# Four w_mod chunks of layer 1 are multiplied between the layers, not inside the delta rule

## The chip, the cores and the metric

The kernel runs on one core of a Trainium2 chip. The metric is the device time of one execution in microseconds. The median of three runs of the kernel before is 1710.85 us (1703.96, 1710.85 and 1711.68).

## What is computed

Two layers run over 640 tokens of width 1024 (128 context tokens, 512 latent ones). Cut to what matters here, for each layer `l`:

```
mod = silu(c) @ w_mod[l] + b_mod[l]           # 6 * 1024 columns: shift1, scale1, gate1, shift2, scale2, gate2
x = x + gate1 * (mixer(rms_norm(x) * (1 + scale1) + shift1) @ w_out[l])
x = x + gate2 * experts(rms_norm(x) * (1 + scale2) + shift2)      # 16 experts, expert choice
```

Layer 0's mixer is an RG-LRU beside differential attention. Layer 1's is a chunked gated delta rule beside grouped-query attention. `scale2` and `gate2` of layer 1 are columns 4096 to 6143 of `w_mod[1]`, and nothing reads them before layer 1's second norm.

## The kernel before, in words

Everything is float32. Activations lie transposed (`xT`, `hT`: 8 tiles of 128 channels by 640 tokens). Each engine has its own hand-written program, and the order in it is the order of the Python code: there is no scheduler.

**Weights.** They pass through nine homes ("slots") of 128 x 4096 floats, 2 MB each. Slots 0 to 2 are the tensor `ring`, and slots 3 to 8 are the first 24576 columns of `arena`. SyncE (SP) issues every weight load, in the order of the list `loads`, in `load_stream`; before a load it waits until TensorE (PE) has read what lay in that slot. A chunk is 512 columns of a weight matrix, 2 MB. `w_mod` has 24 chunks, `all_mods[0]` to `all_mods[23]`. Chunks 20 to 23 are `scale2` and `gate2` of layer 1. In this text "input chunks" are those of `w_in_cd`, layer 1's input projection, taken in the order 4, 5, 0, 1, 2, 3 (chunk 5 is narrower, 1088 KB).

**Experts.** `moe_pe` runs 16 experts. An expert's three matrices take a set of three slots: set 0 is slots 3, 4, 5, set 1 is 6, 7, 8, set 2 is 0, 2, 1. The experts use the sets in the order 0, 1, 2, 0, 1, 2, 0, 1, and then 2, 0, 2, 0, 2, 0, 2, 0. So slots 6, 7 and 8 are free after the eighth expert, and the last expert (the sixteenth) is in set 0. Of each expert, PE runs line 1648 (the first two matrices), 1660 and 1665 (the third). GpSimd (POOL) adds the result to `moe_rows` in DRAM with an indirect DMA (line 1803).

**Between the layers.** After layer 0's last expert, `gather_sum_act` makes ScalarE (ACT) wait for all the adding DMAs (semaphores `y_room0` to `2`), and issue two small cache loads and four loads of `moe_rows`, a quarter of the columns each (`m_quarter0` to `3`), into `rows_m` at column 12800 of the arena. Meanwhile `sum_pe` on PE runs 12 fillers (`keep_busy`, two recorded matmuls each, whose result nobody reads), and then for each of 8 channel tiles five transposes (line 1920); VectorE (DVE) adds the tile to `xT` (lines 1351, 1354), ACT squares it (line 676), and PE sums the squares (line 1926). The norm's root, `norm_spread_pe` (lines 641, 642) and the scaling of `hT` follow, and then the first input chunk (line 762). SP issues the second and third input chunks when `m_quarter3` has come.

**The w_mod chunks.** A chunk's product is eight matmuls with 32 columns each (`mod_rows_pe`, line 493, 16 records for 8 instructions), a copy by ACT, four transposes (`mod_turn_pe`, line 504) and two or three small operations of DVE (`mod_dve`). Chunks 20 to 23 are handled by the `late_mod_*` functions inside `delta_pe`: each of the first four of the delta rule's five rounds takes one chunk, with the first half of its matmuls (`late_mod_rows(.., 0)`, line 522) between `am(j + 2)` and `am(j + 3)`, the second half between `wu(j)` and `wu(j + 1)`, and the transposes (`late_mod_turn`, line 532) behind `wu(j + 1)`.

Of the kernel before, what the change touches and what calls it, by code (L numbers as in the profile page):

```python
# [23 lines left out]
D = 1024  # L24
# [54 lines left out]
def build(nc, io, outs):  # L79
    with ExitStack() as ctx:  # L80
# [35 lines left out]
        def ar(off, *shape):  # L116
            n = 1
            for x in shape:
                n *= x
            assert off + n <= AR, (off, n)  # L120
            v = arena[:, off:off + n]
            if len(shape) == 2:
                v = v.rearrange("p (a b) -> p a b", b=shape[1])
            elif len(shape) == 3:
                v = v.rearrange("p (a b c) -> p a b c", b=shape[1], c=shape[2])
            return v
# [95 lines left out]
        def mmk(pe, out, lhs, rhs):  # L222

            for k in range(KD):
# [11 lines left out]
        chunks = [all_mods[:4] + ins[0][0:1] + all_mods[4:5] + ins[0][1:2] + all_mods[5:6] + ins[0][2:3] +  # L236
                  all_mods[6:8] + ins[0][3:4] + all_mods[8:11] + ins[0][4:5] + all_mods[11:14] + wouts[0][:1] +
                  all_mods[14:15] + wouts[0][1:] + all_mods[15:20],
                  ins[1] + all_mods[20:] + wouts[1]]
        first_slots = [0, 1, 2, 0, 1, 2, 0, 2, 1, 2, 2, 0, 2, 2, 2, 1, 2, 2, 2, 0, 1, 2, 6, 7, 0, 2, 1]  # L240

        SETS = ((3, 4, 5), (6, 7, 8), (0, 2, 1))
# [16 lines left out]
        loads = []  # L259
        for l in range(2):  # L260
            for i, c in enumerate(chunks[l]):
                s = first_slots[i] if l == 0 else i % 3 if i < 6 else i % 2
                slot_uses[s] += 1
                slot_of[c] = (s, slot_uses[s])
                loads.append((c, s, last_in_slot.get(s)))
                last_in_slot[s] = c
            for p, three in enumerate(SETS):
                for s in three:
                    slot_of["exp", l, s] = slot_uses[s]
                    slot_uses[s] += IN_SET[p]  # L270
            loads.append((("experts", l), None, dict(last_in_slot)))
            for s in range(3):
                last_in_slot[s] = ("experts", l)
        slots = [ring[:, s, :] for s in range(3)] + [ar(4096 * s, 4096) for s in range(6)]
        w_here = [S(f"w_here{s}") for s in range(9)]
# [199 lines left out]

        mrow = [ar(22360 + 512 * i, 512) for i in range(2)]
        modsum = sm[:, 616:624]
        mrow += [ar(25856 + 512 * i, 512) for i in range(2)]
        mrow_of = lambda i: mrow[i % 2 + (2 if i >= 14 else 0)]
        MOD_RAW = 26944  # L480

        def mod_rows_pe(pe, i, pair=None):
# [905 lines left out]
        idx_p = ar(26928, NE)[0:CAPP, :].bitcast(U32)  # L1388

        grow_s, grow_p = wr[:, :, :, :].rearrange("p l k e -> p (l k e)"), csil.rearrange("p k c -> p (k c)")  # L1390
        rows_m = ar(12800, NT, D)


        row_of = lambda n: ar(20480 + D * (n % 3), D)
# [416 lines left out]
        def load_stream(sp):  # L1811
            for c, s, prev in loads:
                if c[0] != "experts":
                    if prev is not None:
                        if prev[0] == "experts":
                            l = prev[1]
                            pair = 1 + SETS[2].index(s)
                            last = max(e for e in range(NE) if set_of(e) == 2)
                            sp.wait_ge(pair_full[pair], moe_base[l][pair] + (last + 1) * PER[pair])
                        else:  # L1820
                            read_by_now(sp, prev)
                    if c == chunks[0][1]:
                        sp.wait_ge(S("x_here"), 16 * NT)
                    if c == chunks[1][1]:
                        sp.wait_ge(S("m_quarter3"), 16)
                    src, n = chunk_src(c)
                    sp.dma_start(chunk(c), src.rearrange("(k p) n -> p k n", p=P)).then_inc(w_here[s], 16)
                    if c == chunks[1][2]:
                        layer1_consts_dma(sp)
                    if c == ins[0][0]:  # L1830
                        setup_late_dma(sp)
                        sp.wait_ge(S("zeroed"), 2)
                        setup_gates_dma(sp)
                    if c == wouts[c[1]][1]:

                        filled(sp, ("dyT", ST) if c[1] == 0 else ("cyT", 3))
                        sp.wait_ge(S("caches"), (48, 96)[c[1]])
                    if c in (all_mods[16], wouts[1][1]):
                        l = 0 if c == all_mods[16] else 1
                        for j in range(3):  # L1840
                            load_expert(sp, l, by_itself(0), j, False)
                        if l == 1:
                            for j in range(2):
                                load_expert(sp, 1, by_itself(FIRST.index(1)), j, False)
                else:
                    experts_stream(sp, c[1], prev)
# [45 lines left out]
                        load_expert(sp, l, in_loop(r, q), j, 2)  # L1892


        def gather_sum_act(act, l):
            for p in range(3):
                act.wait_ge(S(f"y_room{p}"), 16 + 16 * IN_SET[p])
            for pair in range(4):
                act.wait_ge(pair_free[pair], moe_base[l][pair] + NE * PER[pair])

            q = S("gqa_cache")
            act.dma_start(gk_c, io["cache_gqa_k"][0, 0].rearrange("t h d -> t (h d)")).then_inc(q, 16)
            act.dma_start(gv_c, io["cache_gqa_v"][0, 0].rearrange("t h d -> t (h d)")).then_inc(q, 16)
            for q in range(4):
                act.dma_start(rows_m[:, :, 256 * q:256 * q + 256],
                              DR["m"][:, 256 * q:256 * q + 256].rearrange("(t p) d -> p t d", p=P))\
                    .then_inc(S(f"m_quarter{q}"), 16)

        def sum_pe(pe, l):
            un = ("nrm", 1, 0)  # L1910
            acc = take(pe, un, 3)
            keep_busy(pe, acc, 12)
            for k in range(KD + 3):
                if k < KD:
                    if k % 2 == 0:
                        pe.wait_ge(S(f"m_quarter{k // 2}"), 16)
                    u = ("ms", l, k)
                    ps = take(pe, u, k % 3)
                    for t in range(NT):
                        last = pe.transpose(ps[:, t * P:t * P + P], rows_m[:, t, k * P:k * P + P], ident)  # L1920
                    finish(last, u)
                j = k - 3
                if j >= 0:
                    pe.wait_ge(S("sq"), 16 + j + 1)
                    for t in range(NT):
                        last = pe.matmul(acc[:, t:t + 1], sq_all[:, j, t * P:t * P + P], ones[:, 0:1],  # L1926
                                         start=(j == t == 0), stop=(j == KD - 1 and t == NT - 1))
            finish(last, un)
# [428 lines left out]
        def delta_pe(pe):  # L2357
# [151 lines left out]
            for i in range(5):  # L2509
                j = 2 * i  # L2510
                for s in range(1, 6):
                    for e in range(2):
                        level_w(j + e, s)

                    if s in (1, 3) and i == 0:
                        kq(TILE_ORDER[2 + s // 2])
                    elif s in (1, 3):
                        state_a(j - 2 + s // 2)
                    elif s in (2, 4) and i < 4:
                        dec(j + 1 + s // 2)  # L2520
                    elif s == 5 and i == 2:
                        kq(ST)
                    for e in range(2):
                        level_x(j + e, s)
                    if s in (1, 3) and i == 0:
                        kk(TILE_ORDER[2 + s // 2])
                    elif s in (1, 3):
                        state_b(j - 2 + s // 2)
                    elif s in (2, 4):
                        qd(j - 1 + s // 2)  # L2530
                    elif s == 5 and i == 2:
                        kk(ST)
                if i < 4:
                    am(j + 2)
                    late_mod_rows(pe, 20 + i, 0)
                    am(j + 3)
                    wu(j)
                    late_mod_rows(pe, 20 + i, 1)
                    wu(j + 1)
                    late_mod_turn(pe, 20 + i, late_row)  # L2540
                else:
                    wu(j)
                    spare()
                    wu(j + 1)
# [36 lines left out]
        def delta_act(act, step):  # L2581
# [55 lines left out]
            for i in range(5):  # L2637
# [26 lines left out]
                uw_read(j)  # L2664
                if i == 4:
                    root(3)
                else:
                    late_mod_act(act, 20 + i, late_row)
                uw_read(j + 1)
            rows_first(8)  # L2670
            square(4)
# [28 lines left out]
        def delta_dve(v, step):  # L2700
# [88 lines left out]
            for i in range(5):  # L2789
# [25 lines left out]
                if i < 4:  # L2815
                    for e in range(2):
                        x_first(j + 2 + e)
                    late_mod_dve(v, step, 20 + i)
            o_sum(v, 9, dscr3, 0)
            o_scale(3)  # L2820
            state_new(8)
# [140 lines left out]
        def _(act):  # L2962
            step = Steps(act, S("act_step"))
            setup_act(act, step)
            for l in range(2):
# [30 lines left out]
                route_act(act, step, l)  # L2996
                moe_act_run(act, l)
                if l == 0:
                    gather_sum_act(act, l)

        @block.vector
        def _(v):
            step = Steps(v, S("dve_step"))
            setup_dve(v, step)
            for l in range(2):
# [35 lines left out]
                route_dve(v, step, l)  # L3041
                moe_dve(v, step, l)
                if l == 0:
                    residual_dve(v, step, l, "ms")

        @block.gpsimd
# [66 lines left out]
```

## Time and profile before

| | us |
|---|---|
| median of 3 runs | 1710.85 |
| the profiled execution's own time | 1709.0 |
| its span in the trace | 1707.2 |
| PE busy | 1571.3 (92%) |
| DVE busy | 667.8 (39%) |
| ACT busy | 426.9 (25%) |
| POOL busy | 253.5 (15%) |

Busy times are of the whole span. Layer 0's experts end near 762 us in the trace, the stretch between the layers goes from there to 802, and the rounds of the delta rule run from about 1120 to 1310. The columns of the window views are, for each engine, busy us and in brackets the instructions; then PE's granted clock as a share of 2.4 GHz (1.00 is 2.4 GHz, 0.50 is 1.2 GHz), the mean busy share of the 16 DMA engines, and GB/s.

### The profile page before, as it was taken

How to read it: one execution, taken by the hardware profiler on the slowest of the kernel's cores; microseconds unless marked ns; L12 is line 12 of the kernel's file. 1: busy time of each engine (PE TensorE's matmuls, PEld its weight loads, DVE VectorE, ACT ScalarE, POOL GpSimd, SP SyncE). 2: the span in 40 equal slices, each digit the busy share in tenths (PEclk: the TensorE clock that was granted, in tenths of full speed). 3: DMA queues.
4: the chain of work that ended last, by engine and by line, in shares of the span. 5: the costliest groups of instructions: out<-in, count | busy, mean ns of one | idle time of the engine just before them, and what ended most of it. 6: DMA issues, size and time to landing. Idle time of an engine off the chain costs nothing.

```text
span 1707.2 us, 39998 instructions
## 1 busy us (share of the span) xinstructions
PE 1571.3 (92%) x17826; PEld 1034.9 (61%) x17826; DVE 667.8 (39%) x1414; ACT 426.9 (25%) x734; POOL 253.5 (15%) x263
## 2 busy tenths in 40 slices
PE   5999998989979999999999989988878998999996
PEld 2554434655546777766655558667666556767774
DVE  3543584751331111113039636644454134222221
ACT  3245413640311111113010236442232032000000
POOL 0000000000011111100000016155452001212211
PEclk8999999999989999997999989999999998999998
DMA  9444444025499999985121100002112617999995
GB/s 345 174 147 167 178 154 105 1 83 213 163 360 367 374 369 365 382 300 167 50 98 51 53 1 2 1 15 88 52 52 77 281 63 276 369 382 362 365 386 193
DMA packets 89932, 325.69 MB, mean 191 GB/s; under 512 B 11556, under 2 KB 17304, under 8 KB 81592
## 3 DMA queue, kind: packets, MB, share of 16 engines
q1 hardware_dynamic: 75824, 284.80, 44.3%
q0 software_dynamic: 9648, 32.65, 7.0%
q10 hardware_dynamic: 4312, 6.03, 1.0%
q8 instruction: 122, 2.00, 0.5%
q14 instruction: 26, 0.21, 0.0%
HBM read 301.30 MB, written 22.16 MB: 189 GB/s over the span
## 4 chain that ended last, share of the span: by engine, by line
PE 73%; DVE 7%; issue 3%; ACT 1%; DMA 1%; POOL 0%; POOLq 0%; DVEq 0%; ACTq 0%
PE pairs L225 19%; PE pairs L1648 17%; PE pairs L1660 7%; PE pairs L1665 3%; PE pairs L1631 2%; PE pairs L371 2%; PE pairs L1264 2%; PE pairs L2416 1%; PE pairs L2210 1%; PE pairs L2190 1%; PE pairs L1278 1%; PE pairs L2173 1%; PE pairs L1926 1%; PE pairs L762 1%; PE pairs L2427 1%
## 5 line engine op out<-in xcount | busy, mean ns | idle before, releaser
L225 PE MATMUL pairs<-hT,ring 128*128 128x128 f32 (+1 forms) x1120 | 306.1, 436 | 2.3 <-ACT hT L385 2.3
L225 PEld LDWEIGHTS pairs<-hT,ring 128*128 128x128 f32 x1120 | 170.6, 192 | 138.3 <-issue 138.2
L385 ACT ACTIVATE arena<-pairs 128x512 f32<-128x512 f32 (+6 forms) x214 | 124.7, 598 | 372.7 <-PE pairs L225 126.6
L1648 PE MATMUL pairs<-arena 128*64 128x80 f32 x5120 | 186.8, 235 | 9.7 <-issue 8.0
L1648 PEld LDWEIGHTS pairs<-arena 128*64 128x64 f32 x5120 | 181.7, 138 | 19.7 <-issue 17.2
L225 PE MATMUL pairs<-ring,hT 128*128 128x512 f32 (+1 forms) x448 | 178.5, 558 | 0.0
L225 PEld LDWEIGHTS pairs<-ring,hT 128*128 128x128 f32 x448 | 84.6, 191 | 90.3 <-issue 87.3
L1723 DVE TENSOR_TENSOR arena<-arena,pairs 128x160 f32<-128x160 f32 x64 | 20.6, 321 | 251.6 <-PE pairs L1648 251.6
L1648 PE MATMUL pairs<-arena,ring 128*64 128x80 f32 x3072 | 111.0, 233 | 5.8 <-issue 5.8
L1648 PEld LDWEIGHTS pairs<-arena,ring 128*64 128x64 f32 x3072 | 107.9, 137 | 12.1 <-issue 12.1
L385 DVE COPY arena<-pairs 128x512 f32<-128x512 f32 (+7 forms) x37 | 25.2, 703 | 127.5 <-PE pairs L225 120.8
L1660 PE MATMUL pairs<-arena 128*64 128x512 f32 x320 | 74.8, 610 | 0.0
L1351 DVE SCALAR_TENSOR_TENSOR xT<-pairs,modt,xT 128x512 f32<-128x512 f32 x24 | 18.0, 750 | 142.1 <-PE pairs L225 124.7
L1688 ACT ACTIVATE arena<-pairs 128x640 f32<-128x640 f32 x32 | 22.5, 704 | 193.1 <-PE pairs L1631 193.1
L1693 ACT ACTIVATE arena<-pairs 128x320 f32<-128x320 f32 x32 | 14.0, 437 | 226.2 <-PE pairs L1648 226.2
L371 PE MATMUL pairs<-cst 128*128 128x512 f32 x110 | 60.8, 698 | 3.2 <-DVE hT L1744 2.3
L676 ACT ACTIVATE arena<-xT 128x640 f32<-128x640 f32 x32 | 23.3, 736 | 157.9 <-DVE xT L1354 138.5
L2139 POOL TENSOR_TENSOR arena<-arena,sm 128x640 f32<-128x640 f32 (+1 forms) x40 | 43.1, 1081 | 93.0 <-DVE sm L2106 93.0
L2842 POOL TENSOR_TENSOR arena<-ring,arena 128x256 f32<-128x256 f32 x60 | 44.0, 750 | 79.4 <-DVE ring L2737 53.6
L493 PE MATMUL pairs<-ring,csil 128*32 128x512 f32 x288 | 42.8, 719 | 10.2 <-DVE modt L593 5.1
L1587 POOL DMA_DIRECT2D h_rows<-arena x10 | 5.4, 538 | 295.7 <-ACT arena L385 295.7
L1772 POOL DMA_INDIRECT hT<-h_rows,arena x32 | 29.5, 923 | 112.1 <-PE pairs L1631 69.0
(410 smaller groups left out, 2255.7 us busy)
## 6 DMA issues: line engine op xcount, KB each, us to landing
arena<-in_exp_w SPq DMA_DIRECT2D x60, 2048.0 KB, 18.8
ring<-in_exp_w SPq DMA_DIRECT2D x36, 2048.0 KB, 18.7
ring<-in_w_mod SPq DMA_DIRECT2D x22, 2048.0 KB, 8.1
ring<-in_w_in_ab SPq DMA_DIRECT2D x5, 2048.0 KB, 13.4
ring<-in_w_in_cd SPq DMA_DIRECT2D x5, 2048.0 KB, 7.9
ring<-in_w_out SPq DMA_DIRECT2D x4, 2048.0 KB, 15.2
h_rows<-arena POOLq DMA_DIRECT2D x10, 512.0 KB, 3.4
arena<-in_w_mod SPq DMA_DIRECT2D x2, 2048.0 KB, 10.0
```

Of the source, the lines that this page charges most:

```text
L225: last = pe.matmul(out, lhs(k), rhs(k), start=(k == 0), stop=(k == KD - 1))
L371: pe.matmul(ps[:, 0:512], ident, cst[:, 0:4, :].rearrange("p a b -> p (a b)"), start=True, stop=True)
L385: return eng.activation(dst, src, ACT.Copy) if eng is nc.scalar else eng.tensor_copy(dst, src)
L493: last = pe.matmul(ps[32 * q:32 * q + 32, 0:512], csil[:, k, :], w[:, k, :], start=(j == 0), stop=(j == 1))
L1264: pe.matmul(ps[:, 0:512], q, k[:, 0:512], start=True, stop=True)
L1631: last = pe.transpose(ps[:, o:o + CAP], xe[p][:, k::KD], ident[0:CAP, 0:CAP])
L1648: last = pe.matmul(lin_of(j, f)[c:c + 64, :], w[:, k, f * P + c:f * P + c + 64], rhs, start=(k == 0), stop=(k == KD - 1))
L1660: last = pe.matmul(y_sample[h], hid[:, f, 0:CAPS], w2[:, f, 512 * h:512 * h + 512], start=(f == 0), stop=(f == FT - 1))
L1665: last = pe.matmul(y_prompt[q], hid[:, f, CAPS:CAP], w2[:, f, 256 * q:256 * q + 256], start=(f == 0), stop=(f == FT - 1))
L1772: g.indirect_dma_start(xe[p], None, DR["h", l], off(e)).then_inc(S(f"gathered{p}"), 16)
L2139: g.tensor_tensor(p, p, rsum(j, e).broadcast_to((P, n)), ALU.mult).then_inc(S("g_norm"), 1)
L2842: g.tensor_tensor(am64(j), a64(j), over_heads(C64[f"level{e}{s}"]), ALU.mult).then_inc(S(f"dl_am{e}"), 1)
```

## The change

Chunks 20 to 23 leave the delta rule. They are loaded ahead of the input chunks, three of them into slots 6, 7 and 8 and the fourth into slot 0, and `sum_pe` multiplies and turns them, with `mod_act` and `mod_dve` on the other engines, ahead of the sum. Eight of the 12 fillers go. The waits and the six DMAs of `gather_sum_act` move from ACT to SP, behind the load of input chunk 4, as `sum_rows_dma`; `rows_m` moves to column 5120. The homes of the other layer-1 chunks move among slots 0 to 2.

```diff
-                  ins[1] + all_mods[20:] + wouts[1]]
+                  all_mods[20:] + ins[1] + wouts[1]]
+        layer1_slots = [6, 7, 8, 0, 2, 1, 0, 2, 1, 0, 1, 0]
...
-                s = first_slots[i] if l == 0 else i % 3 if i < 6 else i % 2
+                s = first_slots[i] if l == 0 else layer1_slots[i]
...
-            for s in range(3):
+            for s in SETS[2] + SETS[1]:
                 last_in_slot[s] = ("experts", l)
...
-        mrow += [ar(25856 + 512 * i, 512) for i in range(2)]
-        mrow_of = lambda i: mrow[i % 2 + (2 if i >= 14 else 0)]
+        mrow += [ar(o, 512) for o in (25856, 26368, 11264, 11776)]
+        mrow_of = lambda i: mrow[i % 2 + (4 if i >= 20 else 2 if i >= 14 else 0)]
...
-        rows_m = ar(12800, NT, D)
+        rows_m = ar(5120, NT, D)
...
-                            pair = 1 + SETS[2].index(s)
-                            last = max(e for e in range(NE) if set_of(e) == 2)
+                            p = next(p for p in range(3) if s in SETS[p])
+                            pair = 1 + SETS[p].index(s)
+                            last = max(e for e in range(NE) if set_of(e) == p)
                             sp.wait_ge(pair_full[pair], moe_base[l][pair] + (last + 1) * PER[pair])
...
-                    if c == chunks[1][1]:
+                    if c == ins[1][1]:
+                        sum_rows_dma(sp, 0)
                         sp.wait_ge(S("m_quarter3"), 16)
...
-                    if c == chunks[1][2]:
+                    if c == ins[1][2]:
                         layer1_consts_dma(sp)
...
-        def gather_sum_act(act, l):
+        def sum_rows_dma(act, l):
...
             acc = take(pe, un, 3)
-            keep_busy(pe, acc, 12)
+            for i in range(20, 24):
+                mod_rows_pe(pe, i, i % 2)
+                mod_turn_pe(pe, i, 2)
+            keep_busy(pe, acc, 4)
...
                 if i < 4:
                     am(j + 2)
-                    late_mod_rows(pe, 20 + i, 0)
                     am(j + 3)
                     wu(j)
-                    late_mod_rows(pe, 20 + i, 1)
                     wu(j + 1)
-                    late_mod_turn(pe, 20 + i, late_row)
...
-                else:
-                    late_mod_act(act, 20 + i, late_row)
...
-                    late_mod_dve(v, step, 20 + i)
...
                 if l == 0:
-                    gather_sum_act(act, l)
+                    for i in range(20, 24):
+                        mod_act(act, i)
...
                 if l == 0:
+                    for i in range(20, 24):
+                        mod_dve(v, step, i)
                     residual_dve(v, step, l, "ms")
```

The order of SP's instructions behind layer 0's experts, before (`in_exp_w` is an expert's matrix, `moe_rows` the summed rows; `s_pair_full1` to `3` are PE's reads of an expert's first, second and third matrix):

```order
L1861 DMA arena<-in_exp_w 128x4x1024
L1889 REGISTER_ALU
L1889 COMPARE_AND_BRANCH
L1827 DMA ring<-in_w_in_cd 128x8x512 [waits s_pair_full1]
L1827 DMA ring<-in_w_in_cd 128x8x272 [waits s_m_quarter3,s_pair_full3]
L1827 DMA ring<-in_w_in_cd 128x8x512 [waits s_pair_full2]
L348 DMA arena<-in_rope 128x4x64
```

and in the changed kernel:

```order
L1864 DMA arena<-in_exp_w 128x4x1024
L1892 REGISTER_ALU
L1892 COMPARE_AND_BRANCH
L1830 DMA arena<-in_w_mod 128x8x512 [waits s_pair_full1]
L1830 DMA arena<-in_w_mod 128x8x512 [waits s_pair_full2]
L1830 DMA arena<-in_w_mod 128x8x512 [waits s_pair_full3]
L1830 DMA ring<-in_w_mod 128x8x512 [waits s_pair_full1]
L1830 DMA ring<-in_w_in_cd 128x8x512 [waits s_pair_full2]
L1905 DMA arena<-in_cache_gqa_k 128x128 [waits s_pair_free0,s_pair_free1,s_y_room2,s_pair_free2,s_y_room1,s_pair_free3,s_y_room0,s_pair_full3]
L1906 DMA arena<-in_cache_gqa_v 128x128
L1908 DMA arena<-moe_rows 128x5x256 x4
L1830 DMA ring<-in_w_in_cd 128x8x272 [waits s_m_quarter3]
```

Four 2 MB loads now stand between the last expert's third matrix and input chunk 4, and the loads of the summed rows stand behind all of them.

On PE, the rounds' end in the delta rule before (L2442 and L2446 are `wu`, L2416 is the next round's `level_w`):

```order
L2446 MATMUL pairs<-arena 64x128 x8
L522 MATMUL pairs<-ring,csil 32x512 x4
L2442 MATMUL pairs<-arena 128x64 [waits s_bank_free6,s_dl_kv1,s_bank_free1,s_dl_vb,s_bank_free3]
L2442 MATMUL pairs<-arena 128x64 x7
L2446 MATMUL pairs<-arena 64x128 x8
L532 MATMUL pairs<-cst,arena 128x128 [waits s_bank_free7]
L532 MATMUL pairs<-cst,arena 128x128 x3
L2416 MATMUL pairs<-hT,arena 64x64 [waits s_bank_free0,s_bank_free1,s_dl_am0]
```

and in the changed kernel:

```order
L2452 MATMUL pairs<-arena 64x128 x8
L2448 MATMUL pairs<-arena 128x64 [waits s_bank_free6,s_dl_kv1,s_bank_free1,s_dl_vb,s_bank_free3]
L2448 MATMUL pairs<-arena 128x64 x7
L2452 MATMUL pairs<-arena 64x128 x8
L2422 MATMUL pairs<-hT,arena 64x64 [waits s_bank_free0,s_bank_free1,s_dl_am0]
```

The second half of the chunk's matmuls and its transposes are gone, and the next round's first matmuls follow the second `wu` at once.

On PE between the layers, in the changed kernel (before, L371's 12 fillers stood in the place of the rows ahead of L1926):

```order
L494 MATMUL pairs<-arena,csil 32x512 [waits s_pair_free0,s_w_here6,s_pair_free3]
L494 MATMUL pairs<-arena,csil 32x512 x7
L505 MATMUL pairs<-cst,arena 128x128 [waits s_pair_free2,s_pair_free0]
L505 MATMUL pairs<-cst,arena 128x128 x3
...
L494 MATMUL pairs<-ring,csil 32x512 [waits s_pair_free1,s_w_here0]
L494 MATMUL pairs<-ring,csil 32x512 x7
L505 MATMUL pairs<-cst,arena 128x128 [waits s_pair_free2,s_pair_free1]
L505 MATMUL pairs<-cst,arena 128x128 x3
L372 MATMUL pairs<-cst 128x512 x4
L1926 MATMUL pairs<-cst,arena 128x128 [waits s_pair_free0,s_m_quarter0]
```

Each chunk waits for its own load (`s_w_here6`, `7`, `8`, `0`), and its transposes wait for ACT's copy; the sum comes behind all four.

## Rows read from the trace of the kernel before

**Rows 1.** The page's chain that ended last, shares by engine.

```profile
PE 73%; DVE 7%; issue 3%; ACT 1%; DMA 1%; POOL 0%; POOLq 0%; DVEq 0%; ACTq 0%
```

**Rows 2.** Windows: the sum at two clocks, and the delta rule's rounds.

```profile
774.54:780.60 6.06, 6.05 (x54) 5.57 (x52) 4.76 (x10) 3.47 (x5) 0.00 (x0) 1.00 0.73 233
780.60:795.00 14.40, 14.31 (x71) 14.22 (x69) 3.03 (x6) 3.76 (x6) 0.00 (x0) 0.50 0.89 286
1120.00:1310.00 190.00, 158.46 (x3608) 128.93 (x3607) 94.56 (x165) 57.79 (x118) 96.43 (x111) 0.98 0.14 48
```

**Rows 3.** The chain between the layers: start us, us, what.

```profile
762.44 12.27 PE pairs L371 x24
...
778.39 0.60 PE pairs L1920 x5
779.00 1.01 PE pairs L1926 x10
...
786.59 8.34 PE pairs L1926 x40
```

**Rows 4.** SP's issues (start us, us), one load's landing, DMA falling idle.

```profile
718.39 11.30 SPq L1861 DMA_DIRECT2D arena<-in_exp_w  x3
733.72 0.39 SPq L1827 DMA_DIRECT2D ring<-in_w_in_cd  x1
...
836.51 0.37 SPq L1827 DMA_DIRECT2D ring<-in_w_in_cd  x1
arena<-in_exp_w SPq DMA_DIRECT2D x1, 2048.0 KB, 22.8
756.00:758.00 2.00, 2.00 (x12) 0.75 (x8) 0.00 (x0) 0.00 (x0) 0.00 (x0) 1.00 0.58 219
```

**Rows 5.** The last adding DMA, ACT's issues, landings of first rows and an earlier add.

```profile
762.66 1.39 POOL L1803 DMA_INDIRECT moe_rows<-hT,arena  x1 [13.55 <-DVE hT L1744]
768.41 2.71 ACTq L1905 DMA_DIRECT2D arena<-moe_rows  x4
arena<-moe_rows ACTq DMA_DIRECT2D x1, 640.0 KB, 4.7
moe_rows<-hT,arena POOLq DMA_INDIRECT x1, 10.5
```

**Rows 6.** Loads of layer 1's experts issued back to back, first and sixth landing.

```profile
1314.81 2.73 SPq L1861 DMA_DIRECT2D arena<-in_exp_w  x5
arena<-in_exp_w SPq DMA_DIRECT2D x2, 2048.0 KB, 11.0
ring<-in_exp_w SPq DMA_DIRECT2D x1, 2048.0 KB, 30.3
```

**Rows 7.** Timeline of PE near the start: w_mod chunks at either clock.

```profile
24.10 3.64 PE L493 MATMUL pairs<-ring,csil 128*32 128x512 f32 x16 [3.17 <-DMA ring<-in_w_mod]
27.68 1.12 PE L504 MATMUL pairs<-cst,arena 128*128 128x128 f32 x4
...
37.68 1.92 PE L493 MATMUL pairs<-ring,csil 128*32 128x512 f32 x16
...
40.38 0.66 PE L504 MATMUL pairs<-cst,arena 128*128 128x128 f32 x4 [0.19 <-ACT arena L385]
```

**Rows 8.** Windows in which the clock falls and returns under the fillers.

```profile
763.50:764.00 0.50, 0.50 (x3) 0.11 (x2) 0.00 (x0) 0.00 (x0) 0.50 (x1) 0.66 0.00 0
...
767.00:767.50 0.50, 0.50 (x2) 0.19 (x1) 0.00 (x0) 0.00 (x0) 0.00 (x0) 0.92 0.02 0
```

**Rows 9.** Delta rule: the chain's chunk rows, and a wait from the timeline.

```profile
1148.18 1.00 PE pairs L522 x8
1151.24 0.59 PE pairs L532 x4
...
1220.76 1.00 PE pairs L522 x8
1145.43 0.27 PE L2403 MATMUL pairs<-arena 64*64 64x64 f32 x1 [0.78 <-POOL arena L2842]
```

## The prediction

> **What bounds the kernel now.** I read the page first. Its chain runs on TensorE for 73% of the span [rows 1], so a change counts only where it shortens or lengthens that chain. Then I read the two places that the change touches. The chain view says what stood on the path, the windows say at which clock, and the timelines of the DMA-issuing queues say when weights can be there.
>
> Between the layers the chain goes through the fillers (762.44 to 774.7) into the sum, with no gap to speak of, and the sum ends at 786.59 + 8.34 = 794.93 [rows 3]. Its first 6 us run at 2.4 GHz and the rest at 1.2 GHz [rows 2]. The fillers cover a wait: the last adding DMA is issued at 762.66, ACT issues the first quarter of the rows at 768.41, and it lands 4.7 us later, at 773.1 [rows 5]. The fillers end 1.6 us behind that, so they bind by a hair. The weight queue is empty then: the last expert's third matrix is the third load from 718.39 on, issued near 729.3; it lands 22.8 us later, at 752.1, and behind it input chunk 4, issued at 733.72, is in near 757.3, in the window in which the DMA share falls to 0.58 [rows 4]. That is 5.2 us for 2 MB. From then until 768 the DMA engines have almost nothing to do, and this is the hole that the change fills.
>
> In the delta rule's rounds PE is busy for 158 of 190 us and the DMA engines for 14% [rows 2]. PE, DVE, ACT and POOL pass a chain to and fro, and the w_mod matmuls stand in PE's part of it [rows 9].
>
> **The change part by part.**
>
> *Delta rule, removed.* Each of four rounds loses two groups of L522 and one of L532. The second L522 group (1.00 us) and L532 (0.59 us) lie on the chain, with PE work directly ahead and behind [rows 9]; the chain has the same pair in all four rounds (1.00, 1.00, 1.00, 0.99 and 0.59, 0.59, 0.59, 0.58). That is 4 x 1.59 = 6.4 us. The first L522 group is free: PE waits another 0.78 us for POOL's mask right behind it [rows 9], and without the group it waits longer. Only in the third round is it on the chain, at 1220.76, but POOL's mask is ready some 0.1 us before it ends, so I count 0.1. ACT's four copies and DVE's dozen small operations go too. They ran while those engines waited for PE, so nothing is counted. Saving: 6.5 us. Bounds: 0, if another engine's chain takes over in every round, and 4 x 2.59 = 10.4, if the first groups counted in full.
>
> *The loads, moved.* Slots 6 to 8 have long been free, so SP issues chunks 20, 21 and 22 at once behind the last expert's matrix (729.7), chunk 23 where input chunk 4 was issued before (733.7), and input chunk 4 some 5 us later. How a deep queue behaves is shown where SP issues the first loads of layer 1's experts: five 2 MB loads go out in 2.73 us, the first two land after 11.0 us in the median and the sixth after 30.3 [rows 6]. From (1315.1 + 11.0) to (1317.6 + 30.3) is 21.8 us for 4.5 loads, or 4.8 us each, in order, and SP is not held up. So the chunks land at about 757.3, 762.5, 767.7 and 772.9, and input chunk 4 at 778.1. Nothing that the last expert needs stands behind them.
>
> *The summed rows, moved.* SP waits for the last adding DMA. Before, that landed by 767.5. With the engines full, such an add took 10.5 us [rows 5], so I put it at 773.2. SP then issues two small loads and the quarters from about 774, before the queue reaches them. The queue delivers in order, so the first quarter comes behind input chunk 4: 778.1 + 0.8 for the add's own bytes + 1.6 for 640 KB = 780.5, with ends 778.3 (4.8 us a chunk) and 782. Queued behind the waiting SP are input chunks 5 and 0 and the constants. They waited for `m_quarter3` before as well and now come some 7 us later. SP's next load waits until PE has read chunk 4, and it was issued at 836.51 [rows 4], so chunk 5 has 40 us of cover; if that went, its 5 us would show. Freeing ACT of 3.5 us of issuing gives nothing, since ACT was waiting.
>
> *PE between the layers, added.* One chunk at full clock is 2.70 us from its first matmul to its transposes, ACT's copy included (37.68 to 40.38), and 0.6 for these: 3.3 us. At half clock it is 3.58 for the matmuls, 0.85 for the copy and 1.1 for the transposes: 5.5 us [rows 7]. At 762.44 the clock is still full; it falls near 763.7, after PE had waited for VectorE, and under the fillers comes back near 767.0 [rows 8]. If it does so here, chunk 20 ends at 766.8, 21 at 770.1, 22 at 773.4, 23 at 776.7 (each landed in time), and the 8 filler records that stay, 0.44 us each, end at 780.2. If the clock never returns, the chunks end at 783.3 and the fillers at 790.3. So the sum starts between 780.5 (the rows) and 790.3. I take 781.5, near the lower end, since PE has work without long holes from 762 on, as it had under the fillers. Before it was 774.7: +7 us.
>
> The Trainium skill has a rule against this change. Its page "TensorE: Matmul & The Clock Gate", section "HAM oscillation — how this bites in real kernels", describes a kernel whose short bursts of matmuls each wait for a DMA, so that the clock falls in the wait and every tile starts cold. By it the first rival below would be the likely case. Our rows show chunk 21 and 22 landed before PE gets to them, so the waits are ACT's copies (0.85 us), not DMAs, and I give the rule a minor chance.
>
> *The sum's pace.* Its work is 40 transposes and 80 one-column matmuls. At full clock that is 40 x 0.12 + 80 x 0.101 = 12.9 us, at half, with the transposes at twice their price, 40 x 0.24 + 80 x 0.209 = 26.3; it took 20.2 [rows 3]. With 8 filler records ahead in place of 24, the stretch at full clock should not grow. I take 1.5 us of it lost, +1.5, with ends -7.3 and +6.1. DVE's and ACT's new operations end before the first quarter is there, and PE's later waits for quarters (1.6 us apart) are shorter than its own 1.6 us steps.
>
> *Sum.* The profiled execution's own time is 1709.0 us, 1.8 below the median of the runs: 1709.0 + 7.0 + 1.5 - 6.5 = 1711.0 us. A measurement of this kernel tells about 0.5% (8.5 us) from no change, so this is no change.
>
> **The rivals.**
>
> 1. *The clock stays low (slower).* PE is at 1.2 GHz through the chunks, the fillers and the whole sum. Price: the sum starts at 790.3 (+15.6) and takes 26.3 us (+6.1); with -6.5 that is +15.2, 1724.2 us. It decides if the clock has not come back when chunk 22's matmuls start. For it: each chunk leaves PE idle for 0.85 us, and the chunk at 24.10 ran at half clock to its end. Against: the one at 37.68 ran at full clock [rows 7], and the fillers from 762.44 on brought the clock back in 4.6 us. This is what the page's rule would give.
> 2. *The delta rule keeps its time.* The rounds are held by the chain of DVE and POOL, and PE only waits longer. Then +8.5, 1717.5 us. Against: behind L532 PE went straight on, and DVE and POOL waited for it.
> 3. *The sum runs at full clock.* With all quarters there sooner after its start, PE's work is denser: 12.9 us instead of 20.2. Then 7.0 - 7.3 - 6.5 = -6.8, 1702.2 us. Against: PE was already busy without holes when the clock fell at 780.6.
>
> **How the numbers follow.** I give the forecast 0.60, the low clock 0.15, the kept delta rule 0.12 and the full clock 0.13. Slower by over 0.5% needs 1717.5 or more: most of the first rival (0.13), half of the second (0.06) and a tail of the forecast (0.02), 0.21. Faster needs 1700.5 or less: a third of the third rival (0.04) and a tail (0.04), 0.08. The rest, 0.71, is within 0.5%. The range takes in the second and third rivals and stops short of the first in full: 1701 to 1721 us.
>
> **What would show it.** Right: in the trace after, the four chunks' matmuls start near 762, 767, 770 and 773, the first L1926 near 781.5, and the sum ends near 803; the last adding DMA lands around 773; the clock falls once inside the sum; the rounds of the delta rule are 6 to 7 us shorter, with L2422 directly behind L2452. Wrong: a PE wait for `m_quarter0` of more than 3 us (the queue is slower than 5.2 us a chunk, or the add lands past 778), L494 at over 3.5 us for the third and fourth chunk (the first rival), new waits for POOL or DVE behind the second `wu` (the second), or a change anywhere else, such as the last two experts slowed by the fuller queue.

## The result, and the profile after

The changed kernel's median is 1718.0 us (1711.8 to 1726.68, 11 runs), against 1709.34 us (1703.96 to 1713.53, 11 runs) of the kernel before. The ratio is 1.0067, 95% interval [1.0049, 1.0084], or +11.5 us with [+8.4, +14.4]; the two medians lie 8.7 us apart. So it is slower, and most likely by more than 0.5%, though the interval begins a hair below that. The time lies in the range (1701 to 1721), but "slower by over 0.5%" was given only 0.21, and the forecast itself, 1711.0, missed by 7 us. The profiled execution took 1726.68 us (span 1724.7); it is the slowest of the 11, so lengths taken from it stand a little high.

Windows of the changed kernel: the stretch in which the chunks are multiplied, the first part and the rest of the sum, and the delta rule's rounds. The columns are those of [rows 2], explained under "Time and profile before".

```profile
757.50:778.50 21.00, 13.76 (x103) 4.03 (x102) 3.17 (x11) 3.16 (x5) 1.39 (x1) 0.81 1.05 387
785.70:790.00 4.30, 4.29 (x37) 3.81 (x36) 3.55 (x8) 2.15 (x3) 0.00 (x0) 1.00 0.45 157
790.00:807.00 17.00, 17.00 (x87) 16.97 (x85) 4.23 (x9) 5.02 (x7) 0.00 (x0) 0.52 0.82 256
1120.00:1310.00 190.00, 159.04 (x3529) 137.13 (x3528) 93.23 (x153) 59.23 (x116) 97.90 (x113) 0.87 0.01 3
```

The last row is the surprise. TensorE (PE) has less to do in the delta rule's rounds, and it is busy as long as before (159.04 against 158.46 us), because its granted clock there fell from 0.98 [rows 2] to 0.87.

Between the layers, PE's timeline of the changed kernel (start us, us, engine, line, operation, in brackets the wait ahead and what ended it):

```profile
762.28 2.50 PE L494 MATMUL pairs<-arena,csil 128*32 128x512 f32 x16 [2.31 <-DVE hT L1745]
765.54 1.12 PE L505 MATMUL pairs<-cst,arena 128*128 128x128 f32 x4 [0.76 <-ACT arena L386]
766.58 3.64 PE L494 MATMUL pairs<-arena,csil 128*32 128x512 f32 x16
...
772.21 1.92 PE L494 MATMUL pairs<-arena,csil 128*32 128x512 f32 x16 [0.55 <-DMA arena<-in_w_mod]
...
777.63 3.35 PE L494 MATMUL pairs<-ring,csil 128*32 128x512 f32 x16 [2.07 <-DMA ring<-in_w_mod]
...
782.26 3.60 PE L372 MATMUL pairs<-cst 128*128 128x512 f32 x8
785.70 2.57 PE L1926 MATMUL pairs<-cst,arena 128*128 128x128 f32 x20
```

Chunk 21's matmuls run at 1.2 GHz (3.64 us): the clock had fallen near 763.5, much as before, but came back only near 770.3 (before: near 767). Chunks 22 and 23 wait for their loads (0.55 and 2.07 us), and after the longer of these waits the matmuls run for the most part at 1.2 GHz again (3.35 us against 1.92). The sum starts at 785.7, not at 781.5. PE shows no wait for the summed rows, but only just: their first quarter was issued at 774.71 and landed 10.0 us later, at 784.7, 1.0 us ahead of the sum.

SyncE's issues in the changed kernel, from its timeline:

```profile
718.25 11.31 SPq L1864 DMA_DIRECT2D arena<-in_exp_w  x3
729.78 26.46 SPq L1830 DMA_DIRECT2D arena<-in_w_mod  x3
756.28 3.99 SPq L1830 DMA_DIRECT2D ring<-in_w_mod  x1
760.32 8.73 SPq L1830 DMA_DIRECT2D ring<-in_w_in_cd  x1
770.50 3.61 SPq L1905 DMA_DIRECT2D arena<-in_cache_gqa_k  x1
774.15 0.51 SPq L1906 DMA_DIRECT2D arena<-in_cache_gqa_v  x1
774.71 8.12 SPq L1908 DMA_DIRECT2D arena<-moe_rows  x4
```

SyncE was held up. Three `w_mod` issues took 26.46 us, where five issues of expert matrices had taken 2.73 [rows 6]. Chunk 23 was issued at 756.3, not at 733.7, and landed at 777.6. The changed kernel's chain shows that landing as what PE had waited for:

```profile
756.28 21.31 DMA ring<-in_w_mod
777.59 0.04 issue
777.63 3.41 PE pairs L494 x16
```

The DMA engines themselves were full (share 1.05 over the first window), and the chunks came some 6 us apart, not 5.2: the last expert's third matrix, issued near 729.3, landed after 24.8 us, at 754, and chunk 23, four loads later, at 777.6. The sum ends at 807.07 in the chain, where it ended at 794.93 before:

```profile
798.74 8.34 PE pairs L1932 x40
807.07 0.02 issue
```

In the delta rule, two steps of PE matter here. `am` is a group of small products on the mask that GpSimd (POOL, line 2842) writes, and `wu` is the two groups of 16 products behind it (L2442 and L2446 before, L2448 and L2452 now). The chain of the changed kernel at the first round's `wu`:

```profile
1158.29 0.74 POOL arena L2842
1159.07 0.27 PE pairs L2409
1159.94 1.90 PE pairs L2448 x16
1161.84 1.90 PE pairs L2452 x16
1163.74 1.90 PE pairs L2448 x16
1165.64 1.21 PE pairs L2452 x9
```

The same four groups took 1.04 and 1.02 us before. They now take the 1.2 GHz price, and no wait for another engine stands between them: PE itself has become slower. The same happens in the second round (from the middle of the first `wu` on) and in the fourth, and not in the third.

First starts read from the traces, as landmarks (one execution each):

| us | before | after | difference |
|---|---|---|---|
| sum's first transpose | 774.5 | 785.7 | +11.2 |
| first matmul of input chunk 4 | 801.9 | 814.5 | +12.6 |
| first `am` of the delta rule | 1116.2 | 1128.7 | +12.5 |
| first transpose behind the rounds (`cyT`) | 1312.4 | 1328.0 | +15.6 |
| rounds, from `am` to `cyT` | 196.2 | 199.3 | +3.1 |

In these two executions the loss arises between the layers and stands unchanged until the rounds, and the rounds give nothing back. The 1.9 us that are left of the 17.5 between the spans come behind them.

### The profile page after: what moved, and what is told of

Read it like the earlier page. It is cut to its first block, busy times and chain, and to the rows that moved or that the text cites. A ratio compares the mean times of both kernels' runs of the same rounds, so it can differ in the third digit from the quotient of the medians.

```text
span 1724.7 us, 39971 instructions
## 1 busy us (share of the span) xinstructions
PE 1579.6 (92%) x17810; PEld 1044.7 (61%) x17810; DVE 667.4 (39%) x1410; ACT 426.5 (25%) x734; POOL 254.0 (15%) x263
## 4 chain that ended last, share of the span: by engine, by line
PE 71%; DVE 7%; issue 3%; DMA 2%; ACT 1%; SPq 1%; POOL 0%; POOLq 0%; DVEq 0%; ACTq 0%
PE pairs L225 19%; PE pairs L1649 16%; PE pairs L1661 6%; PE pairs L1666 3%; PE pairs L1632 2%; PE pairs L372 2%; PE pairs L1265 2%; DMA ring<-in_w_mod 1%; PE pairs L1279 1%; PE pairs L2196 1%; PE pairs L2216 1%; PE pairs L2422 1%; PE pairs L2179 1%; SPq L1830 1%; PE pairs L2433 1%
## 5 line engine op out<-in xcount | busy, mean ns | idle before, releaser
L372 PE MATMUL pairs<-cst 128*128 128x512 f32 x94 | 52.4, 699 | 0.9 <-ACT arena L386 0.9
```

What stands on the lines that cost most here:

```text
L372: pe.matmul(ps[:, 0:512], ident, cst[:, 0:4, :].rearrange("p a b -> p (a b)"), start=True, stop=True)
```

## The experiments

**Theory A.** (Theory B in the expectations is the second rival below.) In the kernel before, the first half of each chunk's matmuls (L522 between `am(j + 2)` and `am(j + 3)`) fills part of PE's wait for VectorE and GpSimd. PE works through the wait and keeps 2.4 GHz for `wu`. Without it the wait is longer and `wu` runs at 1.2 GHz. **The rivals**: the prediction's view (the removal saves 6.5 us, and the loss is all between the layers), and a chain through VectorE and GpSimd that keeps its length.

**The delta rule's part alone (e1).** The kernel before, without loading or multiplying chunks 20 to 23 (and without ScalarE's and VectorE's work on them; it leaves out their result and sets these columns to constants):

```diff
-                  ins[1] + all_mods[20:] + wouts[1]]
+                  ins[1] + wouts[1]]
...
-                    late_mod_rows(pe, 20 + i, 0)
...
-                    late_mod_rows(pe, 20 + i, 1)
...
-                    late_mod_turn(pe, 20 + i, late_row)
```

> The kernel before, with the four late w_mod chunks neither loaded nor multiplied (their columns of the modulation are set to constants): the delta-rule part of the change alone, nothing added between the layers. The theory of the prediction (6.5 us leave the chain): 1709 - 6.5 = 1702.5 us. Theory A (TensorE's clock): the matmuls of the w_mod chunks kept TensorE active enough for 2.4 GHz, and without them the clock falls to 1.2 GHz in the products behind them, as the trace of the changed kernel shows with a mean granted clock of 0.87 from 1120 to 1310 us against 0.98 before; then the rounds keep their time or lose up to 4 us: 1706 to 1713 us, with the clock at 0.9 or below in the rounds. Theory B (DVE's and POOL's chain holds the rounds): 1709 us, with the clock as before.

Measured: 1709.54 us (1703.96 to 1717.52, 12 runs) against 1707.69, ratio 0.9996 [0.9974, 1.0018]. The interval is [-4.4, +3.1] us: taking this work away does not give the forecast's 6.5 us.

**The same, with idle matmuls at the first place (e2).** Four 32 x 512 matmuls whose result nobody reads stand where the first half stood:

```diff
                     am(j + 2)
+                    idle_rows()
                     am(j + 3)
```

> As e1_delta_only, plus in each of the four rounds four matmuls of 32 columns by 512, whose result nobody reads, in the place where the first half of a w_mod chunk's matmuls stood (between the masks' two products, where TensorE waits for POOL anyway). Theory A: the clock stays at 2.4 GHz in the rounds and the saving appears: 4 to 9 us faster than e1_delta_only, about 1702.5 us. Theory B: no change against e1_delta_only.

Measured: 1697.06 us (1695.13 to 1704.28, 8 runs), ratio 0.9931 [0.9902, 0.996]. Added work makes the kernel 12.5 us faster than e1 by the medians (11 us by the two ratios), more than the 4 to 9 expected. The windows of the rounds in e1, and then in e2:

```profile
1120.00:1310.00 190.00, 157.23 (x3486) 136.46 (x3479) 90.60 (x149) 53.08 (x110) 93.99 (x108) 0.88 0.01 3
```

```profile
1120.00:1310.00 190.00, 158.45 (x3483) 128.92 (x3482) 92.95 (x152) 55.06 (x114) 92.69 (x106) 0.96 0.06 20
```

The rounds last 200.7 us in e1's profiled execution and 188.2 in e2's, 12.5 less. That this is the difference of the medians too is in part chance, since e1's profiled execution (1717.52 us) is the slowest of its 12. In e1 the wait ahead of the second `am` is 1.78, 1.97 and 1.66 us in the first, second and fourth round, and `wu` falls to 1.90 us a group in all three. In e2 it is 0.78, 0.74 and 0.66, and `wu` stays at 1.04. In the third round it is 0.84 in both, and `wu` stays at 1.04 in both.

**All the work kept, only its place changed (e9).** The kernel before, with the first half moved next to the second:

```diff
                     am(j + 2)
-                    late_mod_rows(pe, 20 + i, 0)
                     am(j + 3)
                     wu(j)
+                    late_mod_rows(pe, 20 + i, 0)
                     late_mod_rows(pe, 20 + i, 1)
```

> The kernel before, with nothing taken away: in each of the first four rounds of the delta rule the first half of the chunk's matmuls moves from between am(j + 2) and am(j + 3) to directly ahead of the second half. Theory A (the matmuls at the first place keep TensorE's clock up through the wait for GpSimd and VectorE behind them, and so through wu; without them the clock falls there): the same work takes longer, the clock in the rounds falls from 0.98 to about 0.9, and the time rises by 4 to 12 us, to 1711 to 1719. The prediction's view (work there is free, a second-place group is 1.00 us on the path): +1.0 us in each of four rounds less the 0.1 of the third, at most +4 us, with the clock in the rounds at 0.98 as before.

Measured: 1719.78 us (1714.0 to 1721.08, 6 runs) against 1707.94, ratio 1.0067 [1.0041, 1.0092], 11.8 us between the medians. The clock in the rounds is 0.92, and they last 206.4 us, 10.2 more than before. Nothing was taken from or given to any engine, and the moved group's own time on the path is at most 4 us. This excludes the view that the group is free to move, and a chain through VectorE and GpSimd that keeps its length. PE's timeline shows what the moved group had filled. In e9 and in e1 the wait ahead of this `am` is 1.78 us where it was 0.78 [rows 9]:

```profile
1145.92 0.27 PE L2403 MATMUL pairs<-arena 64*64 64x64 f32 x1 [1.78 <-POOL arena L2842]
```

and the chain of e9 goes on with

```profile
1146.65 1.90 PE pairs L2442 x16
1148.55 1.90 PE pairs L2446 x16
1150.45 3.26 PE pairs L522 x16
1153.71 1.04 PE pairs L2442 x16
```

The wait ends at the same GpSimd operation as before, and the two groups behind it cost 1.90 in place of 1.04 and 1.02 us; the clock is back only near the end of the w_mod matmuls.

**The changed kernel, with idle matmuls at the first place (e3), and at all three (e4).**

> The changed kernel (1718 us), plus the same four idle matmuls in the place of the first half in each round. Theory A: the delta rule gets 6 to 9 us shorter and the clock in the rounds goes back to 0.96 or more: 1709 to 1712 us. Theory B: 1718 us.

> The changed kernel, plus idle matmuls and transposes of the same count and shape in all three places of each round, so that the delta rule costs TensorE what it cost before: the between-layers part of the change alone. The traces put it at 12.5 us more than before (the first product of layer 1 starts at 814.5 us against 801.9): 1721.5 us if that is all, by either theory, with the clock in the rounds at 0.96 or more by theory A. If it comes out at 1718 or less, part of the 12.5 us is given back later.

e3: 1709.0 us (1700.83 to 1713.24, 12 runs), ratio 0.9996 [0.9973, 1.0019]. The same four matmuls a round take back 9.0 us by the medians and about 12 by the two ratios (1.0067 and 0.9996); e3 can't be told from the kernel before. The clock in the rounds is 0.93, though, not the 0.96 expected: in the fourth round of e3's profiled execution `wu` ran at 1.90 us a group in spite of the idle matmuls, as in e8's and e10's below. They help, and don't hold the clock in every round. e4: 1715.2 us (1711.19 to 1723.78, 12 runs), ratio 1.0051 [1.0025, 1.0076]. With PE's work of the rounds in its old places, what is left is the price of the stretch between the layers, +8.7 us by the ratio; this is less than the 12.5 expected from the slowest execution's trace. In e4's own trace chunk 23 waited only 0.87 us and ran at full clock (1.92 us), and the sum started at 783.1, 8.6 later than before, behind a wait of 0.44 us for the summed rows. The step from e3 to e4 is the second group and the transposes, 6.2 us by the medians (4 x 1.59 = 6.4 was their price on the path) and about 9 by the ratios.

**The rows ahead of input chunk 4 (e5), and without fillers (e6).** Both are e3 with SyncE's row loads one place earlier:

```diff
+                    if c == ins[1][0]:
+                        sum_rows_dma(sp, 0)
                     if c == ins[1][1]:
-                        sum_rows_dma(sp, 0)
                         sp.wait_ge(S("m_quarter3"), 16)
```

> e3_first_group (1709 us), with the loads of the summed rows issued by SyncE ahead of input chunk 4 instead of behind it. In the changed kernel the last w_mod chunk landed at 777.6 us, its product and transposes ended at 782.4 and the fillers at 785.9, and the first quarter of the rows had landed near 785.2. Theory Q (the queue: the place of the rows behind input chunk 4 costs time): the rows land 5 us earlier, but chunk 23 and the fillers still end at 785.9, so at most 1 us faster: 1708 us. Theory R (the rows are late because of the queue's total, not of their place): 1709 us.

> e5_rows_first without the four fillers ahead of the sum. The sum then starts when chunk 23's transposes are done, 3.4 us earlier (near 782.4 us in the trace). Theory Q: 3 us faster than e5_rows_first, 1705.5 us. Against it: if the fillers kept the clock up for the sum, the sum takes 2 to 3 us longer and the total stays at 1708.

e5: 1706.68 us (1700.03 to 1714.93), ratio 1.0002 [0.9981, 1.0023]; e6: 1706.16 us (1696.44 to 1715.29), ratio 0.9997 [0.9972, 1.0023], with 1706.99 us as the median of before in this group. Neither differs from e3's 0.9996. In e6 the sum starts at 782.3, ahead of e5's 785.0, and that is the fillers' 3.4 us, less 0.8 us by which chunk 23's transposes ended later in e6; what it is worth at the end lies within the intervals. The first quarter of the rows lands at 779.1 in e5 and 779.6 in e6, and the sum starts behind chunk 23 in both, so the earlier rows had nothing to give while chunk 23 and the fillers stood ahead of the sum. Only once the fillers go are they needed: with the rows behind input chunk 4, as in the changed kernel, they landed at 784.7, later than e6's sum starts.

**Fewer chunks between the layers (e7: two, e8: three).** The others stay in the rounds, as before; idle matmuls fill the first place of the rounds that have none, and the rows come ahead of input chunk 4. In e8 SyncE waits besides, ahead of input chunk 5, until PE has read chunk 22.

```diff
+                  all_mods[20:22] + ins[1] + all_mods[22:] + wouts[1]]
...
-            for i in range(20, 24):
+            for i in range(20, 22):
                 mod_rows_pe(pe, i, i % 2)
```

> Only chunks 20 and 21 go between the layers (slots 6 and 7, rows loaded ahead of input chunk 4, four fillers); chunks 22 and 23 stay in the first two rounds of the delta rule, and the third and fourth round have the four idle matmuls in the place of the first half. Chunk 21 lands near 766 us, before the rows can be there (775), so the between-layers part should cost 0 to 2 us against the kernel before (sum starts by 777), and two rounds save 1.6 us each on TensorE's path. Theory A with Q: 1709 - 3.2 + 1 = 1703 to 1707 us. If the stretch between the layers costs what it costs now (11 us), it comes out above 1712.

> Chunks 20, 21 and 22 between the layers, chunk 23 in the first round of the delta rule, otherwise as e7_two_chunks. Chunk 22 landed at 772.2 us in the changed kernel, so its transposes end near 775.6 and the sum starts near 779 with the fillers, 4 us later than before; three rounds save 1.6 us each or more. Theory A with Q: 1704 to 1708 us, within 2 us of e7_two_chunks.

e7: 1699.24 us (1694.19 to 1705.56), ratio 0.9955 [0.9937, 0.9974]; e8: 1702.45 us (1696.66 to 1712.47), ratio 0.9966 [0.9946, 0.9986]. Both beat both kernels, and both are faster than expected (1703 to 1707, and 1704 to 1708); e8 is 3.2 us behind e7. In e7's trace the sum starts 0.7 us earlier than before and takes 18.4 us in place of 20.2, and the rounds last 191.6 us, 4.6 less. Why the sum keeps full clock for longer there was not tested. In e7 PE shows no wait for a chunk's load, and the rows now end the wait, by 0.40 us:

```profile
766.61 1.92 PE L494 MATMUL pairs<-arena,csil 128*32 128x512 f32 x16
769.31 0.66 PE L505 MATMUL pairs<-cst,arena 128*128 128x128 f32 x4 [0.78 <-ACT arena L386]
769.80 3.60 PE L372 MATMUL pairs<-cst 128*128 128x512 f32 x8
773.80 1.31 PE L1927 MATMUL pairs<-cst,arena 128*128 128x128 f32 x10 [0.40 <-DMA arena<-moe_rows]
```

Two chunks fit into the time that the 12 fillers took (the sum starts at 773.8, before at 774.5). The third and fourth do not: the sum starts at 777.1 with three (chunk 22 waits 1.99 us for its load in e8), and near 785 with four.

**The rows issued by ScalarE (e10).** e3, with the waits and the six row and cache DMAs behind ScalarE's copy of chunk 21:

```diff
                     for i in range(20, 24):
                         mod_act(act, i)
+                        if i == 21:
+                            sum_rows_dma(act, 0)
```

> The changed kernel with the idle matmuls at the first place (as in e3), with the summed rows' loads issued by ScalarE, behind its copy of chunk 21, and no longer by SyncE behind input chunk 4. Theory A with its reading of SyncE (its issues block while the queue is full, the one of input chunk 4 until 769, and the rows come behind everything that is queued ahead): the rows are issued at about 770 to 774 here too, since ScalarE waits for the last adding DMA at 770.4, so that the first quarter is there between 776 and 783, ahead of the fillers' end; the sum starts where it does in e3, at 785 within 2 us, and the time is that of e3 and e5, 1706 to 1709. Rival (the move of the waits and issues from ScalarE to SyncE costs several us by itself): the sum starts 3 us earlier or more, and the time is 1703 to 1706. If ScalarE's waiting holds up its copies of chunks 22 and 23, it is the other way: the sum starts 2 to 4 us later.

Measured: 1711.74 us (1706.96 to 1720.24, 12 runs) against 1707.94, ratio 1.0019 [1.0002, 1.0035]. The median stands 3.8 us above that of before, where e3's stood 1.3 above, and the ratio's intervals overlap, so a loss is likely but not settled. The sum starts at 790.3, 5.6 us later than in e3 (from one execution of each; that of e10 is the slowest of its 12). The last case of the expectation is what happened, and larger. ScalarE's timeline in e10:

```profile
768.54 0.60 ACT L386 ACTIVATE arena<-pairs 128x512 f32<-128x512 f32 x1 [2.69 <-PE pairs L494]
771.14 0.34 ACTq L1904 DMA_DIRECT2D arena<-in_cache_gqa_k  x1
771.51 0.46 ACTq L1905 DMA_DIRECT2D arena<-in_cache_gqa_v  x1
772.00 8.35 ACTq L1907 DMA_DIRECT2D arena<-moe_rows  x4
780.45 0.60 ACT L386 ACTIVATE arena<-pairs 128x512 f32<-128x512 f32 x1 [11.31 <-issue]
```

The four issues take 8.35 us where ScalarE had needed 2.71 [rows 5], at a time when the DMA engines are full (share 1.05 from 757.5 to 778.5 here too) and not empty. PE waits 4.67 us for the copy behind them. So issuing from ScalarE at this place wins nothing back, and the move to SyncE is not what cost the time: it keeps such a hold-up away from an engine that computes. The Trainium skill, page "DMA: Bandwidth & Descriptors", section "Issuing engines are not separate DMA queues", says that the time an engine's sequencer spends on starting a DMA is usually small beside the DMA. By that rule the issuer would not matter; this trace is the unusual case, with 8.35 us of issuing for four loads of 640 KB.

## Why the prediction was right or wrong

**The sum of the terms.** It was +7.0 + 1.5 - 6.5 = +2.0. By the runs it is +9 to +11 between the layers and about -1 in the delta rule, each by the ratios. Both parts were too favourable. That the time still lies in the range is luck: the range reached that far because of the second rival, whose mechanism did not occur.

| term | predicted | trace | runs |
|---|---|---|---|
| start of the sum | +7.0 | +11.2 | |
| pace of the sum | +1.5 | +1.0 | |
| the two together | +8.5 | +12.2 | +11.1 (e3's ratio less e2's), +8.7 (e4) |
| delta rule | -6.5 | +3.1 | -0.7 (e1), with [-4.4, +3.1] |

**The step that failed** is in *Delta rule, removed*: "The first L522 group is free: PE waits another 0.78 us for POOL's mask right behind it [rows 9], and without the group it waits longer." The wait did become longer by just that 1.00 us (1.78 in place of 0.78), and the row was read rightly. But I treated the group as work without effect. It kept PE at 2.4 GHz, and without it `wu` falls to 1.2 GHz in three of the four rounds, those in which the wait became longer. The saving on the path is real: at a kept clock (e2) the rounds are 8.0 us shorter than before, in the bounds I gave (0 to 10.4). The loss of clock takes 11 to 12.5 us (e1 against e2). Neither my forecast nor a rival priced a clock that falls in the rounds. The lower bound 0 was argued from another engine's chain, and nothing excluded a loss.

**Start of the sum, mis-sized.** The term was +7.0 and measured +11.2. "SP is not held up" was wrong: I took it from expert matrices, issued at 0.5 us each [rows 6], while the `w_mod` loads blocked SyncE for 26.46 us for three. The chunks landed some 6 us apart, not 5.2, chunk 23 at 777.6 and not at 772.9, and PE fell back to 1.2 GHz in the 2.07 us wait for it. "The 8 filler records that stay ... end at 780.2" became 785.7. Of these 5.5 us, 1.7 are chunk 21 at half clock, 0.55 and 2.07 the waits for chunks 22 and 23, and 1.4 chunk 23's matmuls, less 0.2 by which chunk 20 was early. The last adding DMA took 7.9 us and landed at 770.4, not at 773.2, but the rows behind it landed at 784.7, not at 780.5. So the rows were a second bound only 1.0 us below the first: without the fillers the changed kernel's sum could have started 1.0 us earlier, not 3.4.

**Pace of the sum, right** (+1.0 against +1.5): its first part ran at 1.00 and the rest at 0.52, as before.

**The rivals.** The first (the clock stays low between the layers) did not come: chunk 22's matmuls took 1.92 us, the price at full clock, and its point of decision was this. Chunk 21 ran at half clock (3.64 us) without a wait for a load, since the clock that fell near 763.5 had not come back yet, and chunk 23 for the most part, with 3.35 us of matmuls behind a wait of 2.07 us for its load. By that last row the rule of the Trainium skill (page "TensorE: Matmul & The Clock Gate", section "HAM oscillation — how this bites in real kernels") held for one of the four bursts, the one with the longest wait for a DMA. The second rival, "the delta rule keeps its time", gave 1717.5, half a microsecond from the measured median, for the wrong reason: it named a chain of VectorE and GpSimd, and e2 shows these engines able to go 12.5 us faster. The third (full clock in the sum) did not come.

**What stays open.** The rounds of e3, e5 and e6 are the same instructions and last 192.9, 185.1 and 186.6 us in their profiled executions. In the fourth round `wu` ran at 1.90 us a group in e3 and at 1.04 in the other two, behind the same waits of 2.5 us for VectorE and 0.5 to 0.7 for GpSimd. When the clock falls in a given execution varies, so a single trace tells the rounds' length to some 4 us only, and I lean on the runs; their medians and ratios differ by up to 3 us. It wasn't tried which part of the queue's state blocks an issue.

## What to carry to other kernels

Before work is taken out of a wait because it is "free there", look at PE's clock behind that wait: matmuls that fill a dependency wait may pay for themselves, and in this kernel useless ones in their place were faster than none. Test it in both directions, by taking the work away with and without idle matmuls in its place. And when an engine is to issue loads into a full queue, price the issue by a load of the same shape under the same load, and keep it off an engine that PE waits for.

## What the runs showed of the hardware that was not expected

- Four idle 32 x 512 matmuls in each of four rounds, about 1 us each, made the kernel 12.5 us faster (1709.54 to 1697.06), and real work of the same size, moved out of that wait to a place a few us later, made it 11.8 us slower (1707.94 to 1719.78), of which at most 4 us are the moved work's own time on the path.
- A wait of 0.78 us behind the group left `wu` at 1.04 us; a wait of 1.78 us in the same place was followed by 1.90 us for the same instructions. In the traces of e1, e9 and the changed kernel all nine waits of 1.66 to 1.97 us at this place were followed by groups at half clock; of the waits of 1.11 us or less in the other kernels all but those of the fourth round in e3, e8 and e10 left the clock up.
- SyncE's issue of a 2 MB load took 0.3 to 0.5 us for expert matrices, also when three loads ahead had not landed yet (718 to 729 us), and 1.1, 18.4 and 6.9 us for three `w_mod` loads right behind them in the changed kernel. Two of them blocked it for 19.14 us in e7 as well:

```profile
730.33 19.14 SPq L1831 DMA_DIRECT2D arena<-in_w_mod  x2
```
